# A hybrid decoder layer on eight cores: token mixer in one pass instead of two, block convolution, norm factors applied behind the matmuls, one stream of weight loads

## The reference, cut to what matters

```python
def decoder_layer(x, conv_prev, ...):
    x = x + 0.5 * swiglu_ffn(rms_norm(x, ffn1_norm), ffn1_w_gu, ffn1_w_down)
    mix, v_state, conv_state = token_mixer(rms_norm(x, mix_norm), conv_prev, ...)
    x = x + mix
    x = x + 0.5 * swiglu_ffn(rms_norm(x, ffn2_norm), ffn2_w_gu, ffn2_w_down)

def token_mixer(h, ...):
    ua, va, glu_a, glu_b, gate_a, gate_b = jnp.split(h @ w_in, SPLITS, axis=-1)
    u = gelu(ua); v = layer_norm(gelu(va), ln_v_g, ln_v_b)
    y_a = chunk_spatial_gating(u, v, w_s, b_s) @ w_pa      # 128 x 128 matrix per head and chunk
    g = glu_a * sigmoid(glu_b)
    c = depthwise_conv31(concat(conv_prev, g)) + b_dw
    y_b = silu(layer_norm(c, ln_c_g, ln_c_b)) @ w_pb
    m = sigmoid(gate_a) * y_a + sigmoid(gate_b) * y_b
    return m @ w_out, v_state, conv_state
```

## Time and profile before

| what | value |
|---|---|
| time, three runs of the kernel | 3792.91, 4277.48, 4456.42 us; median 4277.48 us |
| span of the profiled execution, slowest core | 3786.4 us (other cores from 3778.3) |
| PE (matmul) busy | 3510.4 us, 93% |
| DVE busy | 936.8 us, 25% |
| ACT busy | 500.8 us, 13% |
| POOL busy (issue of the weight loads) | 170.1 us, 4% |
| HBM read | 603.16 MB |
| chain that ended last | PE 91%, DVE 4%, ACT 2%, DMA 1%, issue 1% |

### The profile page before, as it was taken

The page is one execution under the profiler, slowest core; times in us unless marked ns, Lnnn a source line. Parts: engine busy times, 40 slices in busy tenths (PEclk is TensorE's granted clock), DMA queues, the critical chain, the costliest instruction groups (busy, mean ns, idle before and its releaser), DMA issues.

```text
span 3786.4 us, 53265 instructions; the slowest of 8 cores (3778.3 to 3786.4 us)
## 1 busy us (share of the span) xinstructions
PE 3510.4 (93%) x22280; PEld 2022.9 (53%) x22280; DVE 936.8 (25%) x1517; ACT 500.8 (13%) x970; POOL 170.1 (4%) x316
## 2 busy tenths in 40 slices
PE   6999999999976999879977998799899999999996
PEld 3666666666645555435545443344466666666663
DVE  5112121121132433331122433211412112112125
ACT  3000000000012111221112112100300000000003
POOL 0000000000000000000000000000000000000000
PEclk7999999999988999989988999899899999999997
...
GB/s 194 67 58 83 64 66 77 60 80 68 60 79 106 89 94 85 50 84 135 135 116 128 117 79 57 101 153 147 68 64 65 78 57 83 68 58 83 64 54 95
DMA packets 50537, 328.44 MB, mean 87 GB/s; under 512 B 6208, under 2 KB 7968, under 8 KB 17248
## 3 DMA queue, kind: packets, MB, share of 16 engines
...
HBM read 603.16 MB, written 14.66 MB: 163 GB/s over the span
## 4 chain that ended last, share of the span: by engine, by line
PE 91%; DVE 4%; ACT 2%; DMA 1%; issue 1%; DVEq 0%; SPq 0%; ACTq 0%; POOLq 0%
PE ps L178 90%; DVE arena L199 2%; ACT arena L184 2%; DVE arena L192 1%; PE ps L181 1%; DMA arena<-xin 1%; DVE arena L382 0%; DMA y<-arena 0%; ACT L184 0%; DVE arena L286 0%; DMA arena<-wst 0%; DVE arena L633 0%; DVE arena L727 0%; DMA arena<-cache 0%; DMA vsamp<-arena 0%
## 5 line engine op out<-in xcount | busy, mean ns | idle before, releaser
L178 PE MATMUL ps<-arena 128*128 128x374 bf16 (+5 forms) x21896 | 3461.8, 319 | 220.7 <-ACT arena L184 117.9
L178 PEld LDWEIGHTS ps<-arena 128*128 128x128 bf16 x21896 | 1974.8, 98 | 1703.9 <-issue 320.4
L192 DVE TENSOR_TENSOR arena<-arena,ps 128x374 bf16<-128x374 f32 (+6 forms) x424 | 221.1, 527 | 1709.5 <-PE ps L178 1175.2
L184 ACT ACTIVATE arena<-ps 128x374 f32<-128x374 f32 (+5 forms) x528 | 246.1, 467 | 2508.6 <-PE ps L178 2508.3
L199 DVE SCALAR_TENSOR_TENSOR arena<-ps,arena 128x374 f32<-128x374 f32 (+3 forms) x451 | 244.0, 547 | 529.7 <-PE ps L178 528.9
L192 DVE TENSOR_TENSOR arena<-arena 128x512 bf16<-128x512 f32 (+5 forms) x198 | 245.0, 1250 | 194.5 <-PE ps L181 161.3
L184 ACT ACTIVATE arena<-arena 128x512 bf16<-128x512 f32 (+9 forms) x277 | 159.9, 612 | 352.4 <-DVE arena L199 180.1
L199 DVE SCALAR_TENSOR_TENSOR arena<-arena 128x374 bf16<-128x374 f32 (+7 forms) x204 | 103.0, 577 | 2.6
L181 PE MATMUL ps<-arena 128*128 128x128 f32 (+4 forms) x384 | 58.4, 306 | 46.7 <-DVE arena L192 14.9
L787 POOL DMA_DIRECT2D arena<-w_gu x88 | 46.7, 531 | 1200.1 <-PE ps L178 1154.2
L181 PEld LDWEIGHTS ps<-arena 128*128 128x128 f32 (+4 forms) x384 | 49.6, 158 | 50.8 <-issue 48.9
...
## 6 DMA issues: line engine op xcount, KB each, us to landing
arena<-w_gu POOLq DMA_DIRECT2D x88, 1024.0 KB, 8.8
arena<-w_dn POOLq DMA_DIRECT2D x64, 704.0 KB, 6.9
arena<-w_glu POOLq DMA_DIRECT2D x32, 1024.0 KB, 7.9
arena<-w_pab POOLq DMA_DIRECT2D x32, 1024.0 KB, 9.3
arena<-w_gate POOLq DMA_DIRECT2D x32, 1024.0 KB, 10.2
arena<-w_v POOLq DMA_DIRECT2D x16, 1024.0 KB, 9.4
arena<-w_u POOLq DMA_DIRECT2D x16, 1024.0 KB, 9.7
arena<-w_out POOLq DMA_DIRECT2D x16, 1024.0 KB, 9.6
```

What stands on the lines that cost most here:

```text
L178: return P.op("pe", lambda e: e.matmul(out, lhsT, rhs, start=start, stop=stop), deps)
L184: return P.op("act", lambda e: e.activation(out=out, in_=in_, func=func, **kw), deps)
L192: return P.op(eng, lambda e: e.tensor_tensor(out=out, in0=in0, in1=in1, op=op), deps)
```

## The change

- **Input and output.** Both are channel-major in HBM now: `xin` comes in three segments (384, 384, 350 tokens; 2 tokens of history fewer), y goes out channel-major; all transposes on PE are gone. X is not kept over the mixer: after FFN1 it is written to HBM (`xsp`, 20 DMAs of ACT's queue) and read back before the output projection. From the output projection on there are 1088 tokens (384, 384, 320); the history is dropped.
- **Norms as an epilogue.** H holds x times gain. The factor 1/rms of each token is multiplied behind the matmul: `gate_part` and `up_part` in the FFN, in `glu_unit`, `u_unit` and the gates by DVE, for v by ACT's scale. The squares are summed while x is produced (`RowNorm.row` behind each down or output block: ACT squares and scales, DVE adds up 15 blocks, 3 matmuls with ones finish a segment). `TokenNorm` does it for the input, matmul by matmul as blocks arrive.
- **Segment by segment.** The last 3 weight tiles of FFN1's last group of down tiles, the last 3 of w_out, and all 8 of FFN2's last group are held, and worked through for segment 0, then 1, then 2. So the norm of a segment can be finished, and for y also multiplied and stored, beside the matmuls of the next one.
- **Mixer in one pass**, in the order glu and convolution, v, u and spatial matrices, gates and projections, output. Each weight is read once. The barriers are gone. The norm of the convolution's output (`ln_phase`, `ln_apply`, `ln_silu`) is put between v tiles.
- **Block convolution.** Tokens are ordered by their position modulo 4. After glu, a block of 128 channels goes to HBM (`gd`) and comes back as 4 groups in which the partitions hold 32 channels x 4 phases; a matrix of 128 x 128 then serves 4 x 4 pairs of tap and phase, so that 9 matmuls of 256 columns (and 9 of 16 for the running sequences) per group do what 31 of 512 (and 31 of 64) did for half of the tokens. The result goes back the same way (`cd`).
- **One weight stream.** `wseq` lists all weight tiles of the program, and `wdone` issues the next load as a slot comes free, whatever stage needs it. PSUM is 6 banks for work and 2 for sums.
- A warm-up of 60 small matmuls stands ahead of the first real one.

The diff, cut to its core:

```diff
+SEG_A = [(0, 384), (384, 384), (768, 350)]
+SEG_B = [(0, 384), (384, 384), (768, 320)]
...
-        banks = Ring([ps[:, b, :] for b in range(8)])
...
+        banks = Ring([ps[:, b, :] for b in range(6)])
+        stat_banks = Ring([ps[:, b, :] for b in (6, 7)])
...
+        def wdone(idx, events):
+            wring.release(idx, events)
+            wissue()
...
+                X = self.Xs[self.s][:, k, 0:n]
+                si, sq, sfree = self.ring.get()
+                self.pend.append((k, si, sq[:, 0:n], act(sq[:, 0:n], X, AF.Square, deps=[dep] + sfree)))
...
+                    self.out[(self.s, k)] = act(self.Hout[:, k, x0:x0 + n], X, AF.Identity, deps=self.hdep + [ev_pv],
+                                                scale=pvc(self.gidx, k))
...
+                            self.ev = tt(self.acc, self.acc, sq, ALU.add, deps=[ea, self.ev])
...
+                        X = self.Xs[s][:, 4 * g:4 * g + 4, 0:n]
+                        e = tt(X, X, RSTD[:, x0:x0 + n].unsqueeze(1).to_broadcast([128, 4, n]), ALU.mult,
+                               deps=[self.rout[s], self.out[(s, 4 * g + 3)]])
+                        P.dma("sp", y_o[:, 4 * g:4 * g + 4, x0:x0 + n], X, "o_y", deps=[e])
...
+            def gate_part(bank, lg, s):
+                x0, n = segs[s]
+                gi_, bg = bank
+                ti, tmp, tfree = TMPS.get()
+                e = tt(tmp[:, 0:n], bg[:, 0:n], RSTD[:, x0:x0 + n], ALU.mult, deps=[lg, rstd[s]] + tfree)
+                banks.release(gi_, [e])
+                return ti, tmp, act(tmp[:, 0:n], tmp[:, 0:n], AF.Silu, deps=[e])
...
+                e = tt(tmp[:, 0:n], tmp[:, 0:n], RSTD[:, x0:x0 + n], ALU.mult, deps=[ea])
+                ed = tt(HID[:, jj, x0:x0 + n], tmp[:, 0:n], bu[:, 0:n], ALU.mult, deps=[e, lu, hid_free[s]])
...
+                        steps = norms[s - 1].last_rows() if s > 0 else []
...
+        def glu_out(c):
+            ev = P.dma("sp", gd[c], GP[c % 3], "gw%d" % (c % 3), deps=[gl[c]])
+            gp_free[c % 3] = [ev]
...
+            for j in range(4):
+                r = P.dma("sp", GPB[c % 3][32 * j:32 * j + 32], gd[c].rearrange("(g c) j n -> j c g n", g=4)[j],
+                          "gr%d" % (c % 3), deps=[gw[c]] + gpb_free[c % 3] + x1_dead)
...
+                    cw[c] = tt(WD[c % 2][:, 2 * h:2 * h + 2].rearrange("p g b (i c) -> p (g b i) c", c=32),
+                               MSKC.unsqueeze(1).to_broadcast([128, 72, 32]),
+                               WP[:, c, 72 * h:72 * h + 72].unsqueeze(2).to_broadcast([128, 72, 32]), ALU.mult,
+                               deps=[cst["wp"]] + wd_free[c % 2] + x1_dead)
...
-                    last_tr = tr(bk[:, kk * 128:kk * 128 + rows], xt[0:rows, k * 128:(k + 1) * 128],
-                                 IDF[0:rows, 0:rows], deps=[lev, c_ev] + bfree)
...
-                    ev = stt(Hout[:, k, l0:l0 + n], X[:, k, x0:x0 + n], PV[:, gidx * 16 + k:gidx * 16 + k + 1],
-                             RSTD[:, l0:l0 + n], ALU.mult, ALU.mult, deps=[er])
...
-                        ea = act(tmp[:, 0:n], bg[:, 0:n], AF.Silu, deps=[lg] + tfree)
...
+                for b in range(9):
+                    mm(bk[:, 0:256], Wd[:, g, b, :], G[:, g, b:b + 256], b == 0, b == 8,
+                       deps=[e_w, sh[c]] + (bfree if b == 0 else []))
+                for b in range(9):
+                    rhs = S[:, g, b, :] if b < 8 else G[:, g, 264:280]
+                    ls = mm(bk[:, 256:272], Wd[:, g, b, :], rhs, b == 0, b == 8, deps=[e_gs])
...
+            wv = P.dma("sp", cd[c], cnp, "cw%d" % ci, deps=[ev])
...
+                r = P.dma("sp", CN[32 * g:32 * g + 32, c].rearrange("p (i n) -> p i n", n=272),
+                          cd[c].rearrange("(i c) g n -> g c i n", i=4)[g], "cr%d" % (c % 4), deps=[wv])
...
+            eg = act(V[0:rows, t, nb * 256:(nb + 1) * 256], bk[0:rows, 0:256], AF.Gelu_apprx_tanh,
+                     deps=[lm, rv_ev] + after, scale=RV[0:rows, t:t + 1])
...
-                for k in range(31):
-                    lc = mm(bc[:, 0:512], DG[:, k, :], GPB[:, k:k + 512], k == 0, k == 30,
-                            deps=st["ready"] + (bcfree if k == 0 else []))
...
+                if len(v_stats) > 4:
+                    v_stat(*v_stats.pop(0))
+                run_steps(side, 1)
...
+            v_ev[t] = ts(V[0:rows, t, :], V[0:rows, t, :], RS[0:rows, t:t + 1], NM[0:rows, t:t + 1], ALU.mult,
...
+                rl[(s, mg)] = P.dma("sp", X2[s][:, 4 * mg:4 * mg + 4, :],
+                                    xsp[s][:, 4 * mg:4 * mg + 4, 0:SEG_B[s][1]], "xr%d_%d" % (s, mg),
+                                    deps=[lya, lyb, lgb, sp_ev[s]])
...
+                    norm2[s].row(mp * 2 + mi, x2f[(s, mp * 2 + mi)])
...
-                    er2 = stt(X[:, k, x0:x0 + n], X[:, k, x0:x0 + n],
-                              PV[:, PV_FIN * 16 + k:PV_FIN * 16 + k + 1], RSTD[:, l0:l0 + n], ALU.mult, ALU.mult,
-                              deps=[er])
```

1516 lines of the change are left out of this document (903 added, 613 removed).

## The result

| | kernel before | changed kernel |
|---|---|---|
| time, four runs each | 3791.68, 3792.91, 4277.48, 4456.42 us | 3254.96, 3256.10, 3256.97, 3257.22 us |
| median | 4035.19 us | 3256.53 us |
| profiled execution, slowest core | 3786.4 us | 3255.7 us (others from 3239.1) |

The ratio of comparable runs is 0.8589, with a 95% interval of 0.8576 to 0.8603.

The account below looks back on a forecast made before the run. PE's streamed columns bound the dense stretches, with PE waiting or slow between them. Stage terms summed to 3235 us, plus 20 for unnamed waits gave a 3255 span; with 6.5 above it, 3262. Range 3215 to 3850.

Parts of the forecast that it names:

- the likeliest case: Whole kernel: the time comes as summed from the stages, 3262 us, within 3215 to 3345; chance 0.56.
- 5 for the last unit behind the last block: Start: PE needs about 5 us for the last unit after the last block loads, so loading ends at 61 us.
- The bounds of 16 to 60: Start: ends given for its net cost, taken as 28 us; 60 if only half of the FFN1 work hides.
- a third to spare: Glu and convolution: DVE's 14.0 us of work per block fits into PE's 20.6 us, with a third left over.
- Some 20 us are there: Trip through HBM: blocks are used one block later, leaving some 20 us for store and loads, so it costs nothing.
- The slow side of the forecast: Rival: trip through HBM not hidden once longer than PE's block; about 3580 us, chance 0.02, or slower than before, 0.02.
- The term for the nine normalisations: v's norm before u: nine DVE operations over 2048 elements, sticking out by some 9 us or vanishing; 4 us taken.
- The 5 us for late down tiles: FFN2's last group: five down tiles are issued only when it begins, so 5 us of waiting, ends 0 and 15.
- The 20 us for waits without a name: Whole kernel: 20 us added for small waits that couldn't be named, at some fifteen changes between stages.
- Slower dense stretches: Rival: dense stretches run slower in the measured execution than in the profile, 3722 to 3894 us; chance 0.27.
- DVE as the bound: Rival: DVE becomes the bound in the mixer, at 1.6 times the rates taken, about 3370 us; chance 0.09.
- Stretches that stay: Rival: in-order engine waits bring back the stretches between stages, 30 us at each of six changes, about 3440; chance 0.04.

Follow-up runs that it names:

- the run with them twice: Changed kernel with the DVE product that builds the convolution's weights done twice: 3297.69 and 3298.46 us.
- the second tile early: Changed kernel with the second gate-and-up tile's load released at segment 0's first x block, the third's at segment 1's: 3263.04 to 3265.17 us, ratio 0.8607.
- all three edits: Changed kernel with gate-and-up tiles released earlier, DVE adding 12 squares for FFN2's last two segments, and row-sum matmuls spread out: 3254.23 to 3258.76 us, ratio 0.8589.

## Why the prediction was right, point by point

The time was 3262 for 3256.5, and the likeliest case came in. It was right for its reasons in most terms, and in three places because errors cancelled. That 3255 met 3255.7 is luck: one term was 19 too low, and an allowance without a reason made up for it.

**Start: mis-sized, 28 us for 47.** The step that failed is "5 for the last unit behind the last block". FFN1's rate is 15.155 us per gate-and-up tile and 10.42 per down tile, 44 x 15.155 + 32 x 10.42 = 1000.3, so the start keeps 1047.7 - 1000.3 = 47.4 (FFN1 itself is 4.7 under the 1005 taken). The loads were done when I said, at about 61 us. PE was not: behind the last block of x stands not one unit of 5 us but three, one for each tile, with the sums 112 matmuls. And DVE comes late to that x. Its first quarter had landed by 50.39 us, when the weight load that waits for it went out; DVE, in its own order, copies it at 68.94, behind the factor and the products of segment 1. PE's timeline, and the window behind the loads:

```profile
1.47 6.09 PE L201 MATMUL ps<-arena 128*128 128x128 bf16 x60 [1.47 <-DVE arena L221]
17.01 9.70 PE L201 MATMUL ps<-arena 128*128 128x384 bf16 x48 [9.45 <-DMA arena<-w_gu]
...
31.94 8.15 PE L201 MATMUL ps<-arena 128*128 128x384 bf16 x32 [5.23 <-DMA arena<-w_gu]
...
69.48 19.57 PE L201 MATMUL ps<-arena 128*128 128x350 bf16 x112 [3.69 <-DVE arena L210]
```

```profile
60.00:85.00 25.00, 20.85 (x118) 12.24 (x117) 10.41 (x27) 9.79 (x22) 0.60 (x2) 0.86 0.04 7
```

At 60 us 7 GB/s are moved and PE is behind its data, not the data behind PE. It begins its work at 17.0 us, waits 5.2 for the second tile, and runs its first 48 matmuls at 9.70 / 48 = 202 ns, against 162.8 by the formula for 384 columns, as the granted clock is 0.50 in the first 3 us. It is 0.50 again from 31.94 to 35.00 (then 0.56 to 38.00) and from 69.48 to 73.00 (then 0.73 to 77.00). These slow stretches cost about 7.5 of the 19.4 us that the term was too low. The three first tiles end at 89.1 us (69.48 + 19.57, the last row), 28 us behind the loads for the 5. The bounds of 16 to 60 held. The 60 small matmuls of the warm-up end at 7.56 us, and the 9.45 us of waiting behind them end at a clock of 0.50, so nothing here shows that they help; the kernel without them was not run.

**Glu and convolution: right, 334 for 336.9.** Matmuls of 256 and 16 columns together are 4.84 us per block for the 5.47 taken. The narrow ones cost 25.2 ns for 37; the waits at the first blocks are 10 us for 4 (2.6, 3.5 and 4.0), and the clock behind them costs 6.5, which the prediction had at nothing. 77.4 for the convolution, 242.7 for glu, 10.1 and 6.5 are 336.7. One error offsets the other. On core 0 the wait of 4.0 is the only one of the three. The stated reason for no loss to DVE was too generous: busy 13.0 us per block for the 14.0 predicted, but not "a third to spare". With its own waits of 2.9 us the room is about 4 us per block, less than one more set of products (4.6); the run with them twice shows both.

**The trip through HBM: right to cost nothing, on a margin.** "Some 20 us are there" was the right cover. The landings of 280 KB and less are 15.9 us together. The slow side of the forecast stands: doubled trips, a chain of about 28 us, cost 143 us at least, so the mechanism is real. That it sets in near 20 us wasn't measured; nothing between 16 and 28 was run.

**v, norms, u: 266 for 272.2.** v is better than forecast, 110.7 ns a matmul (15.94 us for a tile of 144) for 115 to 116.5. The 116.5 of the earlier trace rows was a mean over a piece that begins slowly. The windows of the kernel before:

```profile
1122.00:1128.00 6.00, 5.78 (x28) 4.12 (x29) 0.08 (x1) 1.67 (x2) 0.00 (x0) 0.50 0.00 0
1128.00:1197.00 69.00, 68.78 (x614) 60.08 (x612) 2.74 (x5) 14.63 (x39) 3.70 (x7) 1.00 0.57 107
```

The first 28 matmuls run at a granted clock of 0.50, the level of 1.2 GHz, after PE had waited for the norm; the other 614 take 69.0 / 614 = 112 ns. So part of the gain in v is that no norm stands ahead of it. Against that stand waits of 9.4 us for the 4 taken: 3.95 ahead of the row sums, whose bank is released behind a reciprocal of 1088 elements on DVE (L218), 3.47 for v's norm, 1.05 and 0.92. The clock behind the first two costs another 3.4.

The term for the nine normalisations had been taken between 0 and 9. The group by shape, which answers to the operation missing in the earlier trace rows:

```profile
L210 DVE TENSOR_SCALAR arena<-arena 128x2048 bf16<-128x2048 bf16 x8 | 5.9, 805 | 0.1
```

One takes 805 ns, not 2292. The Trainium skill (VectorE: DVE Perf Modes, The perf-mode tier table) has 693 ns. The trace stands 16% above that and far below my upper bound.

**Gates, output, FFN2, end: 1602 for 1598.9.** The gates are one piece of the chain, 472.07 us for 3072 matmuls (1656.79 to 2128.86).

The 978 for FFN2's body was scaled from FFN1's row of 1007; FFN2's own row, 998, would have given 969. At the rates of the trace (14.745 us per gate-and-up tile, 10.14 per down tile) it is 44 x 14.745 + 32 x 10.14 = 973, so here too an error of 5 covers something else. The 5 us for late down tiles were 0; in their place PE waits 3.34 and 3.12 us for the halves of the sums, with 3.2 us of lower clock behind them. Behind the last down block the end is 15.2 us: the reciprocal 2.15 and four products 5.69, as taken, the store of 640 KB lands in 4.0 for 5.

**The 20 us for waits without a name** were needed: the stages together are 20.7 over their terms, 14.7 of it in start and FFN1 (19.4 less 4.7), 6 in v, norms and u. So the allowance covered a mis-sized term more than it did waits at changes of stage. There is one cause that no term but the start's had: the lower clock behind each wait, an estimated 20.6 us over the program. The sum took every matmul behind a wait at the price of the dense stretches.

**The rivals.** Slower dense stretches: all four runs hold a granted clock of 0.990 to 0.994, so this case did not come in. That is in part luck. The versions with the second tile early and with all three edits, both within 7 us of the changed kernel, had executions of 3885.99 and 3879.08 us, with the cores of one die at 0.809 to 0.815, and my second case was 3722 to 3894. The Trainium skill (TensorE: Matmul & The Clock Gate, Part 1) says 13/16 for dense all-core matmuls; in these four runs the trace does not agree, while the clocks listed for those two executions do. DVE as the bound: not here, but about 4 us per block away from it. Stretches that stay: six barriers put back 34 us and the convolution's norm behind v 62, so what closed them is mostly where the norms stand; for the other norms it is not shown.

**The signs.** Most came as named: no gap over 10 us, a span near 3255, a block of 20.0 us for 20.6, fewer HBM reads. Four did not. The chain names PE for 93%, not 97. It has pieces on gd (12.70 and 12.36 us at the first block), which I had called a sign of being wrong; PE itself waits there for 3.5 us, since a chain follows a whole trip back when only its last part is waited for. DVE is busy for 19.48 of the 20 us from 1423 to 1443, in v, over my 90%, and PE loses nothing by it there. And PE is not without a gap: eight of 2.6 to 4.0 us stand between 60 us and the end. One reading was off without consequence: DVE's lowest share in a dense window is 15%, not 12.

**What wasn't tried**: norms ahead of the matmuls in the new kernel, which alone would price the epilogue in FFN1 and FFN2. Nor were the layout of x and y, the two passes, the single stream of weight loads or the warm-up put back one at a time; their shares are read from the table of stages only.
